# Two blocks made one, convolution taps spread anew, turned probabilities copied first, and a routing with early scatters and a list that skips, in a two-block fp32 model

## What is computed

```python
def first_block(x, ...):
    z = rms_norm(h, ln_g) @ w_in                      # seven parts of width 1024
    c_val, c_glu, c_gate, hq, hf, hi, hg = jnp.split(z, split_pts, axis=-1)
    y_conv = conformer_conv_branch(...)               # 31 taps, norm, w_pw2
    y_hgrn = hgrn2_branch(...)                        # 8 heads, decays, state
    h = h + jnp.concatenate([y_conv, y_hgrn], -1) @ w_out
    pe = p @ w_pp
    gate = jax.nn.sigmoid(rms_norm(h, pe_norm_g) @ w_pg)
    return rms_norm(h + gate * pe, final_g)

def rg_lru(x, wa, ba, wx, bx, lam):
    ...
    log_a = -LRU_C * r * jax.nn.softplus(-lam.astype(jnp.float32))
    ...

def second_block(x, ...):
    u = rms_norm_2(h, norm_mix_g)
    x_rnn, g_rnn, q_c, kv_c, k_pe, gate_logits = jnp.split(u @ w_in, ...)
    xa = causal_conv(x_rnn, conv_w, conv_b)           # 4 taps
    ya = rg_lru(xa, ...) * jax.nn.gelu(g_rnn)
    yb = mla(q_c, kv_c, k_pe, positions, ...)         # softmax over blocks of keys, 16 heads
    merged = gates[:, :, 0] * ya + gates[:, :, 1] * yb
    h = h + merged @ w_out
    return h + hier_moe(rms_norm_2(h, norm_ffn_g), ...)

def hier_moe(x, ...):      # top group, top two of its 8 experts
    ...
    def expert_block(args):                           # 128 rows of one expert
        xb, e = args
        hb = jax.nn.silu(xb @ w_gate[e]) * (xb @ w_up[e])
        return hb @ w_down[e]
```

## Time and profile before

| | us |
|---|---|
| median of 3 runs (lowest to highest) | 3026.41 (3025.27 to 3027.02) |
| the profiled execution | 3029.65 |
| its span | 3027.8 |
| PE busy (share of the span) | 2735.9 (90%) |
| PE's weight loads | 2158.8 (71%) |
| DVE busy | 1649.6 (54%) |
| ACT busy | 1233.3 (41%) |
| POOL busy | 202.8 (7%) |
| mean DMA rate over the span | 109 GB/s |
| mean granted TensorE clock | 0.962 |

### The profile page before, as it was taken

How to read it: one execution, slowest core, us unless ns; L and a number is a source line. 1 busy time by engine, 2 the same in 40 slices (tenths; PEclk the granted TensorE clock), 3 DMA queues, 4 the chain that set the end, 5 groups by cost and what they waited for, 6 DMA issues and landing times. The chain is left out here.

```text
span 3027.8 us, 33758 instructions
## 1 busy us (share of the span) xinstructions
PE 2735.9 (90%) x12640; PEld 2158.8 (71%) x12640; DVE 1649.6 (54%) x2524; ACT 1233.3 (41%) x1734; POOL 202.8 (7%) x183
## 2 busy tenths in 40 slices
PE   7999999999999999979999988998989889389993
PEld 5877777777777787757777788676767668357772
DVE  5677777767741314433334323666666653456664
ACT  4243443344340314534424424545555541246661
POOL 0010111101100000000000000000000000522113
PEclk9999999999999999989999999999999999699997
DMA  5322212232244220022122020000000130979996
GB/s 176 131 88 101 101 70 101 101 101 77 88 152 172 80 84 35 36 63 63 33 65 62 28 82 22 23 15 23 15 23 15 56 80 35 334 284 345 357 370 259
DMA packets 168688, 329.06 MB, mean 109 GB/s; under 512 B 17831, under 2 KB 125480, under 8 KB 154840
## 3 DMA queue, kind: packets, MB, share of 16 engines
q1 hardware_dynamic: 152952, 289.25, 27.6%
q0 software_dynamic: 14720, 34.64, 3.0%
q10 hardware_dynamic: 864, 3.15, 0.3%
HBM read 293.94 MB, written 100.16 MB: 130 GB/s over the span
## 5 line engine op out<-in xcount | busy, mean ns | idle before, releaser
L398 PE MATMUL PS<-UHI,WHI 128*128 128x512 f32 x1008 | 416.4, 413 | 16.9 <-DVE arena L820 12.8
L398 PE MATMUL PS<-ULO,WHI 128*128 128x512 f32 x1008 | 402.3, 399 | 0.0
L398 PE MATMUL PS<-UHI,WLO 128*128 128x512 f32 x1008 | 402.0, 399 | 0.0
L127 DVE TENSOR_TENSOR WLO<-arena,WHI 128x1024 fp32r<-128x1024 f32 x96 | 117.8, 1228 | 271.3 <-ACT WHI L123 271.0
L398 PEld LDWEIGHTS PS<-UHI,WHI 128*128 128x128 f32 x1008 | 192.1, 191 | 68.7 <-issue 21.7
L398 PEld LDWEIGHTS PS<-ULO,WHI 128*128 128x128 f32 x1008 | 192.2, 191 | 46.3 <-issue 4.1
L398 PEld LDWEIGHTS PS<-UHI,WLO 128*128 128x128 f32 x1008 | 191.5, 190 | 46.5
L1454 PE MATMUL PS<-U2HI,WHI 128*128 128x512 f32 x512 | 207.0, 404 | 13.2 <-DVE WLO L127 13.2
L1454 PE MATMUL PS<-U2HI,WLO 128*128 128x512 f32 x512 | 203.1, 397 | 0.0
L1454 PE MATMUL PS<-U2LO,WHI 128*128 128x512 f32 x512 | 203.1, 397 | 0.0
L834 DVE SCALAR_TENSOR_TENSOR RC<-arena,cols,RC 128x1024 f32<-128x1024 f32 x120 | 157.4, 1312 | 9.9 <-issue 0.4
(11 more groups left out here) (451 smaller groups left out, 5872.7 us busy)
## 6 DMA issues: line engine op xcount, KB each, us to landing
arena<-in_w_in SPq DMA_DIRECT2D x88, 512.0 KB, 3.9
xd_dram<-in_x SPq DMA_DIRECT2D x32, 768.0 KB, 5.8
y_dram<-in_x SPq DMA_DIRECT2D x32, 768.0 KB, 6.2
arena<-in_w_gate SPq DMA_DIRECT2D x13, 1024.0 KB, 7.2
arena<-in_w_up SPq DMA_DIRECT2D x13, 1024.0 KB, 11.3
arena<-in_w_down SPq DMA_DIRECT2D x13, 1024.0 KB, 13.9
arena<-in_w_out SPq DMA_DIRECT2D x32, 256.0 KB, 2.9
RB<-in_w_gate SPq DMA_DIRECT2D x7, 1024.0 KB, 7.2
```

The costliest lines, as they stand in the source:

```text
L127: return eng.tensor_tensor(dst, src, hi.bitcast(F32), ALU.subtract)
L398: last = pe.matmul(o[:, h * HALF:(h + 1) * HALF], x[:, k, :], y[:, k, h * HALF:(h + 1) * HALF], start=(k == r == 0), stop=(k == ND - 1 and ...
```

## The change

Four parts that touch different stages.

1. **Taps.** The same 31 taps per head, placed elsewhere among the updates and splits.
2. **One block.** The gate block and the recurrent block become one, without the barrier. The first two weight tiles of the recurrent products have buffers of their own (`FRAW`, `FHI`, `FLO`) in token rows 8 to 13, loaded by SP once six token tiles are stored; ACT and DVE split them at the last steps of the gate loop. PE runs the first half (512 of 1024 columns) of products 1 and 0 ahead of the last `turn_u`, which goes to banks 4 and 5 instead of 0 and 1, and then the second halves. The softplus constants are computed at the start of this block, on DVE and ACT, ahead of the first splits of `w_out`.
3. **Attention.** `turned(g, n)` runs ahead of `largest(g, n + 2)`.
4. **Routing.** The first eight scatters no longer wait for the last normalized tile nor stand behind the zeroing of XB. Weights of expert 1 wait for all scatters, of 2 to 4 for the rows of experts 0 to 2. The list's 16 scatters move into the expert loop, two per pass in the first eight passes, with a bounds check at the list's length, out of which rows are skipped; the list's load stands in the eleventh pass.

```diff
@@ the head loop, DVE @@
                     decayed_queries(i)
+                    taps(c, 0, 1)
                     lower(n + 2)
-                    taps(c, 0, 3)
+                    taps(c, 1, 3)
                     if i:
                         head(i - 1)
+                    taps(c, 3, 5)
                     update(i, 1)
                     masked(i, 0)
                     masked(i, 1)
                     lower(n + 3)
-                    taps(c, 3, 5)
                     update(i, 2)
                     centre(i)
                     masked(i, 2)
                     taps(c, 5, 8)
                     update(i, 3)
                     masked(i, 3)
+                    taps(c, 8, 11)
                     lower(n + 4)
-                    taps(c, 8, 10)
                     update(i, 4)
                     norm(i)
                     masked(i, 4)
+                    taps(c, 11, 14)
                     lower(n + 5)
-                    taps(c, 10, 11)
                     update(i, 5)
                     masked(i, 5)
-                    taps(c, 11, 14)
+                    taps(c, 14, 17)
                     update(i, 6)
                     masked(i, 6)
+                    taps(c, 17, 20)
                     lower(n + 6)
-                    taps(c, 14, 16)
                     update(i, 7)
                     masked(i, 7)
-                    taps(c, 16, 18)
-                    taps(c, 18, 22)
+                    taps(c, 20, 24)
                     lower(n + 7)
                     state(i)
-                    taps(c, 22, 26)
-                    taps(c, 26, CONV_K)
+                    taps(c, 24, 27)
+                    taps(c, 27, CONV_K)
@@ gate and recurrent block, SP @@
                     sp.dma_start(x1_dram[m], HTOK[:, m, :]).then_inc(s_x1st, 16)
+                    if m == 5:
+                        sp.wait_ge(s_x1st, 16 * 6)
+                        for n in range(2):
+                            load(0, n)
                 sp.wait_ge(s_x1st, 16 * NT)
+                sp.wait_ge(s_u2n, NT)
+                for n in range(2, NX):
+                    sp.wait_ge(s_rwlo, n - 1)
+                    load(0, n)
...
@@ PE @@
+                def project(b, n, halves=(0, 1)):
+                    if halves[0] == 0:
+                        pe.wait_ge(s_rwlo, NX * b + n + 1)
+                        if n >= 2 or not isinstance(b, int):
+                            pe.wait_ge(s_revac, NX * b + n - 1)
+                    o, w = banks(2 * (n % 2)), weight_of(b, n)
+                    for h in halves:
...
+                pe.wait_ge(s_gsig, NT - 1)
+                project(0, 1, (0,))
+                pe.wait_ge(s_u2lo, NT - 1)
+                project(0, 0, (0,))
                 turn_u(NT - 1)
+                pe.wait_ge(s_u2lo, NT)
+                block_of(0)
@@ DVE, ahead of the output product @@
                 dve.tensor_copy(PFEAT[:, 0, :], banks(4)).then_inc(s_pfeat, 1)
+                lam = cols[:, :, ROWS["lru_lambda"]]
+                dve.tensor_scalar(CREC[0], lam, -1.0, 0.0, ALU.mult, ALU.max)
...
+                dve.wait_ge(s_softexp, 2)
...
+                dve.tensor_scalar(crec, CREC[0], -8.0, None, ALU.mult)
+                dve.drain()
                 dve.wait_ge(s_x3, 16)
@@ ACT, in the gate loop @@
+                    if s == NT - 1:
+                        weight_hi(0, 0)
+                        weight_hi(0, 1)
@@ DVE, in the gate loop @@
+                    if s == NT - 1:
+                        weight_lo(0, 0)
+                        weight_lo(0, 1)
                 turned_lo(NT - 1, s_u2hi, U2LO, U2HI, s_u2lo)
@@ attention, DVE @@
                     for n in range(NTASK):
+                        turned(g, n)
                         if n + 2 < NTASK:
                             largest(g, n + 2)
-                        turned(g, n)
@@ experts, SP @@
-                    if b < 2:
+                    if b == 0:
                         sp.wait_ge(s_h2p, NT)
+                    elif b == 1:
+                        sp.wait_ge(s_scat, 16 * 2 * NT)
                     elif b < NRW:
-                        sp.wait_ge(s_scat, 16 * 2 * NT)
+                        sp.wait_ge(s_xland[b - 2], 16)
@@ routing, POOL @@
-                pool.wait_ge(s_h2p, NT)
-                for k in range(3):
-                    last = pool.memset(XB[k], 0.0)
-                last.then_inc(s_xzero, 1)
                 for n, (m0, m1) in enumerate(BATCHES):
+                    if n == 1:
+                        pool.wait_ge(s_h2p, NT)
+                        for k in range(3):
+                            last = pool.memset(XB[k], 0.0)
+                        last.then_inc(s_xzero, 1)
                     pool.wait_ge(s_rows8, n + 1)
...
-                for u in range(2):
-                    for m in range(NT):
-                        pool.indirect_dma_start(list_dram, bass.IndirectOffsetOnAxis(ap=LISTROW[:, u, m:m + 1], axis=0),
-                                                PARKI[:, u, m:m + 1], None).then_inc(s_listst, 16)
-                pool.wait_ge(s_listst, 16 * 2 * NT)
-                pool.dma_start(LISTI[:], list_dram[0:NOVER * P].rearrange("(b p) o -> p (b o)", p=P)).then_inc(s_listed, 16)
-                pool.wait_ge(s_listed, 16)
+
+                def list_tokens(m):
+                    for u in range(2):
+                        pool.indirect_dma_start(list_dram[0:NOVER * P, :],
+                                                bass.IndirectOffsetOnAxis(ap=LISTROW[:, u, m:m + 1], axis=0),
+                                                PARKI[:, u, m:m + 1], None, bounds_check=NOVER * P - 1,
+                                                oob_is_err=False).then_inc(s_listst, 16)
...
                 for b in range(NS):
+                    if b < NT:
+                        list_tokens(b)
+                    elif b == NT + 2:
+                        pool.wait_ge(s_listst, 16 * 2 * NT)
+                        pool.dma_start(LISTI[:], list_dram[0:NOVER * P].rearrange("(b p) o -> p (b o)", p=P)
+                                       ).then_inc(s_listed, 16)
                     if 3 <= b + 3 < NE:
                         rows_in(b + 3)
                     elif b + 3 == NE:
+                        pool.wait_ge(s_listed, 16)
                         pool.wait_ge(s_xgt, NE - 2)
                         gather(XB[NE % 3], LISTI[:, 0:1], s_xover)
```

495 lines of the change are left out of this document (244 added, 251 removed).

## The result

| | before | changed |
|---|---|---|
| median, us (lowest to highest) | 3025.84 (3019.85 to 3027.02), 4 runs | 2914.35 (2912.22 to 2916.78), 4 runs |
| ratio, 95% interval | | 0.9636 (0.9619 to 0.9652) |
| profiled execution / its span, us | 3029.65 / 3027.8 | 2912.40 / 2910.4 |

The change makes the kernel 3.6% faster, by 111 us; the forecast was 2916. The table takes eight marks from PE's timeline in both profiles (the start or end of the same matmul) and says between which of them the 117.25 us went by which the two profiled executions differ (all but 0.4 of them ahead of the last mark).

The account below looks back on a forecast made before the run. PE was taken as the bound nearly everywhere, its idle time the prize. Terms -49.9 - 16.0 - 16.0 - 28.6 = -110.5 took 3029.65 to 2919.2 us, 2916 with the median 3.2 lower; range 2902 to 2946.

Parts of the forecast that it names:

- The taps: First block's head loop: 43.9 us of PE's waits for DVE go, plus 6 us of lost clock; term -49.9 us.
- the rival that the loop keeps part of its waits: Head loop: half of the 43.9 + 6 us stays, giving 2941 us; chance 0.14.
- The seam: Between gate and recurrent block: halves fill PE's idle time around the last turn; -22.4 us, bounds -17 and -23.
- The constants: Softplus constants ahead of the output product: their 5.1 us paid in full, with restart at half clock +6.4 us.
- The attention: Copy of turned probabilities ahead of the search: 1.0 us sooner at each of 16 places; term -16.0 us.
- The rival that nothing is won there: Attention: the exponential sets the pace, so nothing is won, giving 2932 us; chance 0.05.
- The first rows: Experts' start: last scatter lands by 2603.7, first gather takes 7 us, PE starts at 2611.5; -12.0 us.
- the rival that they come no sooner: Experts' start: scatters land as slowly as in full queues, so -12.0 falls away, giving 2928 us; chance 0.10.
- The second wait: Experts' start: PE's 15.01 us wait behind list writes and the list's load goes; -15.0, and -1.6 for half-clock restart.
- the list doesn't skip: Expert loop: rows out of range are written after all, costing some 5 us, giving 2921 us; chance 0.03.
- slower: Expert loop turns from PE-bound to DMA-bound; giving all back needs 247 GB/s in place of 332, 3032 us; chance 0.02.
- POOL: Rival: POOL bounds the first eight experts at 12 us each instead of 10.2, giving 2930 us; chance 0.04.

## Why the forecast was right, and where it wasn't

- **Bound.** That PE is the bound, and its idle time the whole prize, held in each stage.
- **The taps**, forecast 49.9, measured 56.2. All 43.9 us of waits went, with no overrun, and with them the rival that the loop keeps part of its waits: each of the first seven heads now takes 88.0 us (from turn of keys to turn of keys). The clock was taken at 6 and was 5.6 in that execution. What the sum lacked was a term: some 0.25 us that each wait costs on top of its length, 6.7 us, worked out as the remainder of two profiles.
- **The seam**, forecast 22.4, measured 22.4. The halves and the last turn come as it was worked out: halves' end 1257.6 less gate's end 1245.5, then turn and splits. That the number fits to the tenth is luck. The term for the clock behind the last pause was 0.5 us; this profile had nothing to pay there, and seven of the nine with the same seam paid 1.3 to 2.7. The run with the one block alone gained 19.7.
- **The constants**, forecast 6.4, measured 3.9 at the first product and 0.5 behind it. "The 5.1 is paid in full" was too much: DVE had 0.84 us of idle time ahead of the first split, and the chain took 4.5 us here. The slower restart behind the longer wait cost no more than the 0.5.
- **The attention**, forecast 16.0, measured 14.1 from its first score product on. 17.1 us of waits went, 1.07 for each of the 16 places. "That fits with some 0.2 to spare" failed: the score products' waits for ACT grew by 6.0 us, 20 times instead of 5, and 4.6 us of short gaps went. The rival that nothing is won there fell.
- **The first rows**, forecast 12.0, measured 11.2; the rival that they come no sooner fell. By the prediction's own terms (landing at 2603.7, gather 7) PE would start at 2610.7, not at 2611.5, so its 12.0 should have read 12.8. The scatter's landing came as taken (4.4 for 4.5 us); the gather beside 3 MB of weights took 8.7 us, not 7, and it is no faster with them held until the scatters have landed (8.8 without). Only the run that holds them until the first rows have landed shortened it, to 4.4 (2517.02 to 2521.46).
- **The second wait**, forecast 15.0 and 1.6 of clock, measured 16.5 in the expert stage. Between executions with the same routing that stage differs by up to 5 us, so the match to the tenth says little.
- **The list's skip** was the step whose price was furthest off. The rival "the list doesn't skip" was put at 5 us; without the skip it is 52. The mechanism of the rival "slower", an expert loop that DMA bounds, is what that run shows, with 223 GB/s in the stretch with the list's writes; it was to decide from 247 down. It stayed away only because the skip works.
- **POOL** didn't bound: its list writes took 0.99 us each, and the rows were there in time. Six gathers of the changed kernel's loop took 2.02 us instead of 1.03; each began 0.11 us into a split of 1.21 us on DVE and took about the rest of that split longer. No row came late by it. The Trainium skill (SBUF — State Buffer, "SBUF: two separate sides") says that whichever of the two starts first has the shared port for its whole instruction, with two SBUF inputs on DVE only against a POOL operation that reads SBUF, a condition that the prediction left out. The trace agrees with the wait for the rest of one instruction, 1.0 us. It doesn't show the near 10 us for an expert that the prediction drew from the rule: one gather in an expert was held up, not all four DMAs.
- **The sum.** By the two profiled executions the change gained 117.25 us, and the forecast had 110.5: 6.3 more in the taps and 2.0 less to pay for the constants, 1.8 less in the attention, 0.8 less in the first rows, and 1.1 ahead of the first mark and behind the last that nobody forecast. That the predicted time lies 2 us from the median, and not 5 to 7, is luck: the profiled execution of before was 3.2 us slower than its median, that of the changed kernel 2 faster.

## What to carry to other kernels

A wait of the engine that bounds costs more than its length: some 0.25 us here each time, and in some executions a stretch at half clock, so one profile of a seam can flatter it by 2 us or more. When work is put ahead of other work to free a waiting engine, look for the one place where the wait is: one swap in eight made the whole gain here, and the other seven only changed which waits PE had. A bulk of scattered 4-byte writes takes rate from the other transfers, 223 instead of 362 GB/s here, unless most of them are skipped. Its place and its skip had to come together here: the skip alone left a wait of 13 us, and the place alone cost 52 us.

## What the runs showed that was not expected

- 2048 scattered 4-byte numbers, two scatters per expert in eight experts, cut the DMA rate from 362 to 223 GB/s and stretched a weight load's landing from 10 to 50 us. The packet counts of the profile don't show whether rows were skipped.
- The drop of TensorE's clock behind one and the same wait of 2 us came in two executions of four in full (6.8 us of the head loop), once in part (1.7) and once not at all. At the pause of 2.4 us in the new seam it came in seven executions of nine.
